# GpSimd rounds the weights' high parts by a converting copy instead of a multiplication by one

## The reference, cut to what matters

```
h = RMSNorm(x);  p = h @ W_in                  # 2048 x about 7980 columns
p -> z | RWKV-7 | mLSTM | MLA | differential attention   (four groups of 512 columns)
y = concat(beta_A*A, beta_B*B, beta_C*C, beta_D*D) * silu(z)
x = x + y @ W_out                              # 2048 x 2048
```

## Time and profile before

| | us |
|---|---|
| median of three runs | 2374.88 |
| lowest, highest | 2373.36, 2375.26 |
| the profiled execution's own time | 2377.48 |
| its span, first to last instruction | 2375.7 |
| mean granted TensorE clock in it | 0.996 |

### The profile page before, as it was taken

The page is one execution under the profiler, slowest core; times in us unless marked ns, Lnnn a source line. Parts: engine busy times, 40 slices in busy tenths (PEclk is TensorE's granted clock), DMA queues, the critical chain, the costliest instruction groups (busy, mean ns, idle before and its releaser), DMA issues. The chain is left out here.

```text
span 2375.7 us, 38650 instructions
## 1 busy us (share of the span) xinstructions
PE 2317.2 (98%) x16160; PEld 1747.8 (74%) x16160; DVE 1131.5 (48%) x1491; ACT 659.4 (28%) x1181; POOL 1729.0 (73%) x1228
## 2 busy tenths in 40 slices
PE   7999999999999999999999999999999999999999
PEld 5767777777777777777777677777777777777777
DVE  5023335646454763555250323557365547635552
ACT  5222222212221232343341223222122212223421
POOL 3677688768577788888537666878586787898784
PEclk9999999999999999999999999999999999999999
DMA  4623243333234445632445233533232243456333
GB/s 156 189 81 101 88 148 105 94 89 113 84 92 125 133 129 168 239 94 74 144 118 158 80 115 89 157 94 99 69 112 89 82 147 111 133 193 217 87 80 124
DMA packets 164335, 285.09 MB, mean 120 GB/s; under 512 B 28664, under 2 KB 36216, under 8 KB 162624
## 3 DMA queue, kind: packets, MB, share of 16 engines
q1 hardware_dynamic: 108352, 180.93, 27.5%
q10 hardware_dynamic: 55808, 101.69, 12.4%
HBM read 230.89 MB, written 51.64 MB: 119 GB/s over the span
## 5 line engine op out<-in xcount | busy, mean ns | idle before, releaser
L738 POOL TENSOR_SCALAR w_hi<-raw 128x512 fp32r<-128x512 f32 x552 | 898.9, 1629 | 444.9 <-PE ps_proj L779 383.9
L748 POOL TENSOR_TENSOR w_lo<-raw,w_hi 128x512 fp32r<-128x512 f32 (+1 forms) x640 | 834.3, 1304 | 154.2 <-ACT w_hi L1243 98.7
L779 PE MATMUL ps_proj<-h_hi,w_hi 128*128 128x512 f32 (+1 forms) x1760 | 738.2, 419 | 7.7 <-ACT stage L1233 4.4
L779 PE MATMUL ps_proj<-h_lo,w_hi 128*128 128x512 f32 (+1 forms) x1760 | 689.9, 392 | 0.0
L779 PE MATMUL ps_proj<-h_hi,w_lo 128*128 128x512 f32 x1728 | 676.8, 392 | 0.0
L779 PEld LDWEIGHTS ps_proj<-h_hi,w_hi 128*128 128x128 f32 (+1 forms) x1760 | 330.2, 188 | 125.9 <-issue 33.3
L779 PEld LDWEIGHTS ps_proj<-h_lo,w_hi 128*128 128x128 f32 (+1 forms) x1760 | 330.1, 188 | 74.2
L779 PEld LDWEIGHTS ps_proj<-h_hi,w_lo 128*128 128x128 f32 x1728 | 326.4, 189 | 68.0 <-issue 11.4
L794 PE MATMUL ps_proj<-w_hi,h_hi 128*128 128x512 f32 x448 | 181.0, 404 | 0.4 <-POOL w_lo L748 0.4
L794 PE MATMUL ps_proj<-w_hi,h_lo 128*128 128x512 f32 x448 | 174.9, 390 | 0.0
L794 PE MATMUL ps_proj<-w_lo,h_hi 128*128 128x512 f32 x448 | 174.5, 390 | 0.0
(11 more groups left out here) (353 smaller groups left out, 3068.0 us busy)
## 6 DMA issues: line engine op xcount, KB each, us to landing
raw<-in_w_in_dram SPq DMA_DIRECT2D x480, 256.0 KB, 2.7
raw<-in_w_out_dram SPq DMA_DIRECT2D x128, 256.0 KB, 3.0
projected<-stage ACTq DMA_DIRECT2D x116, 256.0 KB, 3.0
arena<-projected ACTq DMA_DIRECT2D x90, 256.0 KB, 3.5
out_dram<-arena ACTq DMA_DIRECT2D x7, 1024.0 KB, 4.7
gated_hi<-arena ACTq DMA_DIRECT2D x24, 256.0 KB, 2.5
gated_lo<-arena ACTq DMA_DIRECT2D x24, 256.0 KB, 3.0
h_hi<-gated_hi SPq DMA_DIRECT2D x8, 768.0 KB, 5.7
```

The lines of the kernel that those rows point to most:

```text
L738: nc.gpsimd.tensor_scalar(hi, src, 1.0, None, ALU.mult).then_inc(s_hi_split, 1)
L748: nc.gpsimd.tensor_tensor(lo, src, hi.bitcast(F32), ALU.subtract).then_inc(s_raw_split, 1)
L779: last = mm(ps_proj[rows, m, :], lhsT, rhs, start=(k == 0 and j == 0), stop=(k == KT - 1 and j == len(products) - 1))
```

## The change

GpSimd's instruction that writes the high part becomes a copy whose output has the type fp32r, so that it converts; the semaphore, the wait behind it, the operands and their shapes stay the same.

```diff
                         if HI_FIRST <= n < HI_LAST:
-                            nc.gpsimd.tensor_scalar(hi, src, 1.0, None, ALU.mult).then_inc(s_hi_split, 1)
+                            nc.gpsimd.tensor_copy(hi, src).then_inc(s_hi_split, 1)
                             pool.wait_ge(s_hi_split, of * (HI_LAST - HI_FIRST) + n - HI_FIRST + 1)
                         else:
```

## The result

The changed kernel took **2381.5 us** (median of six runs, 2379.6 to 2385.8) against 2374.7 (six runs, 2373.4 to 2375.3): 6.8 us slower. The ratio of the runs is 1.0035, with a 95% interval from 1.0025 to 1.0045. The forecast was 7.3 us faster. The time lies inside the stated range and on the other side of no change. Its profiled execution took 2379.6 us, one of its two fastest; that of the kernel before, 2377.5, is above all six of its runs. So the two traces show only 2.1 of the 6.8 us.

What follows compares the result with a forecast made beforehand. TensorE bounds the kernel, with GpSimd hidden behind its steps. 1.3 us of direct waits plus 6.0 us from VectorE's shorter chains make 7.3 us, taking the median 2374.9 to 2367.6 us; range 2360 to 2392.

Steps and rivals of the forecast that it cites:

- What bounds the kernel: TensorE, busy 2317.2 of 2375.7 us; only its 58.5 us without a matmul, including waits for VectorE and ScalarE, could change.
- The 19.4 us of the prediction: Sum of TensorE's six larger waits for VectorE and ScalarE past the setup, of which 31% was to go.
- rival B: GpSimd's copy is longer than the multiplication and GpSimd becomes the bound: 2400 us with a 1.89 us copy; chance 0.23.
- The copy's duration: GpSimd's copy of a 128x512 tile, taken as 1.0 us against the multiplication's 1.49; ends 0.56 and 1.89.
- The direct waits: TensorE's waits on GpSimd's split, 0.9 and 0.4 us: a shorter copy returns at most 1.3 us.
- The step that failed: VectorE waits out whole GpSimd instructions; average delay falls from 0.52 to 0.36 us, 31% less, with a shorter copy.
- The 6.0 us of gain: In TensorE's waits behind VectorE's chains: 31% of 19.4 us saved; ends nothing and half of the 19.4.
- Rival D: Copy moves each subtraction's place, so a critical chain can meet more; at worst 2374 us, its chance counted within 0.27.
- Rival A: VectorE's chains before TensorE's waits don't shrink, meeting the subtraction instead: only 1.3 us saved, 2373.6 us; chance 0.27 with others.

Runs made afterwards that it cites:

- one pause: The changed kernel with one GpSimd memset of the low part's buffer (512 columns) between copy and subtraction: 2413.8 us, ratio 1.0171.
- two pauses: The changed kernel with two GpSimd memsets (512 and 256 columns), each waited for, between copy and subtraction: 2381.7 us, ratio 1.0030.
- the copy outside and inside: Against the kernel before, copy only outside steps 68 to 275 of each layer: 2369.7 us; only inside them: 2389.7 us; multiplication elsewhere.
- finer pieces: Against the kernel before, copy only outside steps 68 to 275 of each layer, plus steps 203 to 211 and 252 to 267: 2365.6 us, ratio 0.9967.
- without the subtraction: Low part written as a copy of the raw tile; high part by copy as changed: 2349.4 us; by multiplication as before: 2346.2 us.

## Why the prediction was wrong

**What bounds the kernel** was read rightly in the main: the differences come through TensorE's waits for VectorE and ScalarE. Past the first 22 us these add up to 31.2 us before and 35.7 after, 51.6 with one pause and 29.1 with two, 24.4 and 39.0 with the copy outside and inside, 22.6 in finer pieces, 15.0 and 11.4 without the subtraction (copy, multiplication). Only the kernel with two pauses stands out of the order of the times. The 19.4 us of the prediction had left out, among smaller ones, L931 (1.7 us) and those at L850 and L856 where the second layer begins (2.8 us).

What it did not see is TensorE's clock. TensorE's busy time moved by some 10 us in the kernels whose times moved most (2307 to 2328 us in all), and behind some of its waits the clock is at 1.2 GHz, so that such a wait costs more than its length. The six runs of the changed kernel have a mean granted clock of 0.995 to 0.997, the 28 runs of the kernel before that were taken beside the experiments 0.997 to 0.999, 0.0016 more in the mean. As an estimate, TensorE being busy throughout, that is 0.0016 x 2380 = some 4 of the 6.8 us. How much of it follows from the longer waits alone was not measured.

**The copy's duration** was estimated at 1.0 us and is 0.61 undisturbed, 0.71 in the mean. The lower of the two numbers that I had worked out, 0.74 from the subtraction less one read, was right; GpSimd's slow multiplication said nothing about its copy. The page's figure of the Trainium skill (GPSIMD Engine Reference, section 3.1), 769 ns for 512 elements in a tight loop, was closer than my choice too; the copy is faster still. With the right size my sum would have come out further on the wrong side, so this is not the step that failed.

**The direct waits** went as predicted, from 1.3 to 0.4 us, a gain of 0.9.

**The step that failed** is the one on VectorE: "An instruction that arrives at a random moment waits on average for the sum of squared durations over twice the period." It has two errors. First, it lets the multiplication hold VectorE for its whole length. The trace of before already showed otherwise: in the middle of the multiplication VectorE's instructions take 0.69 us. I had looked at one line's mean (L1668, 1.221 us), found that the formula gave the same number, and taken that for a test. It was a coincidence of place: 18 of the 32 instructions at L1668 began in a subtraction, and 6 in the changed kernel. Had I split the instructions by what GpSimd was doing when they began, as in the table above, the saving in hold would have been near zero instead of 31%, and near zero it was (520 us in both traces). Second, the arrivals are not random. In a chain of VectorE the two engines lock into a pattern, and what a chain costs depends on how many of its instructions fit between two subtractions. The multiplication's idle length was useful, as room for one unheld instruction; the copy took that room away. The 6.0 us of gain became a loss that came to 6.8 us in all. That the time still lies inside the stated range is luck: the range reached up to 2392 us for rival B's longer copy, which did not come.

**Rival D** described the mechanism almost as it is, a copy that moves each subtraction so that a chain meets more of them, and then priced it at nothing, on the ground that as many waits grow as shrink. By place, the profiled execution has -7.1 (without the 0.9 before the first step ends) and +10.0 us. But the long chains with the most two-input instructions are on the losing side, and that I could have seen, since their pattern stands in the trace of before. I also cited the rule (Trainium skill, SBUF — State Buffer, "Who interferes with whom": whichever starts first holds the shared pair for the whole instruction) as if the trace agreed throughout. It agrees for the subtraction, 1.65 us with over 1 us of it left; for GpSimd's one-input instructions the measurement differs, 0.3 us of hold out of 1.49 or 0.61, and decides.

**Rival B** needed a copy of over 1.6 us and is out. **Rival A** foresaw that VectorE's chains would not shrink, but not that they could lengthen.

## What to carry to other kernels

Before shortening an instruction on an engine that shares a port, split its neighbour's durations by what the shared engine was doing when they began: only the part in which it really holds the neighbour can be won, and its harmless part can be the room in which the neighbour works. Where two engines alternate in long chains, count how many instructions fit between two blocking ones; averages over the span say nothing about it. A change whose total is near zero may be the sum of larger gains and losses by place, and a comparison step by step shows which places to keep: here that turned a loss of 6.8 us into a gain of 8.5.

## What the runs showed of the hardware that I had not expected

A one-input fp32 instruction of GpSimd on 128x512 holds a two-input instruction of VectorE by 0.29 us (0.98 against 0.69) if that begins with over 1.25 us of the multiplication left, or with 0.25 to 0.5 us of the copy's 0.61, and the multiplication's last 1.0 us does not hold it. A two-input one holds it to its end (1.66 us). A memset on GpSimd (0.53 us for 512 columns) does not hold it: in the kernel with one pause 19 instructions begun in one took 0.69 us in the mean, and in that with two pauses 113 took 0.71, as beside an idle GpSimd. On the other side, GpSimd's own instructions stretch beside VectorE's chains: the multiplication from 1.49 to 1.93 us, the subtraction from 1.29 to 1.62.

GpSimd's converting copy is 2.4 times as fast as its multiplication by one, 611 against 1492 ns by the median, and takes less than half of the subtraction's 1290; and yet the fastest kernel here that still subtracts keeps the slower instruction for 366 of the 552 steps.

TensorE's clock fell from 2.4 to 1.2 GHz (granted clock 0.50) behind single waits of 1.9 to 2.5 us in the examples above, for 3.4 us each time, but not behind every one: with two pauses it fell behind the wait of 1.93 us that ends at 1104.7 us and not behind the equal one that ends at 1059.0. In the trace with one pause eleven such stretches end before the last microseconds, in that of before five.
